# mLSTM layer: one merged query-key map instead of two, and gate products in four 32-column groups

## The reference, cut to what matters

```python
def mlstm_branch(u, conv_w, conv_b, w_q, w_k, w_v, w_gates, b_gates, mh_norm_w, skip_w):
    c = jax.nn.silu(centred_depthwise_conv(u, conv_w, conv_b))
    q = headwise(c, w_q)
    k = headwise(c, w_k)
    v = headwise(u, w_v)
    qkv = jnp.concatenate([q, k, v], axis=-1)
    gates = jnp.einsum('bsc,ncg->nbsg', qkv, w_gates) + b_gates      # 2 directions x 8 gates
    ...
    s = jnp.einsum('bhtd,bhsd->bhts', qj, kj) * jnp.exp(log_D - m_t[..., None])
    ...
    out = h * mh_norm_w + skip_w * c
```

## Time and profile before

| | |
|---|---|
| time, median of 3 runs | 1830.76 us (1828.91 to 1831.51) |
| the profiled execution | 1830.13 us, of it 1828.3 us span |
| TensorE (PE) busy | 1692.8 us, 93% of the span |
| VectorE (DVE) busy | 1047.2 us, 57% |
| ScalarE (ACT), GpSimd (POOL) busy | 585.4 us, 575.0 us |
| mean granted TensorE clock | 0.974 of full |

### The profile page before, as it was taken

The page is one execution under the profiler, slowest core; times in us unless marked ns, Lnnn a source line. Parts: engine busy times, 40 slices in busy tenths (PEclk is TensorE's granted clock), DMA queues, the critical chain, the costliest instruction groups (busy, mean ns, idle before and its releaser), DMA issues.

```text
span 1828.3 us, 20608 instructions
## 1 busy us (share of the span) xinstructions
PE 1692.8 (93%) x8180; PEld 1339.7 (73%) x8180; DVE 1047.2 (57%) x1503; ACT 585.4 (32%) x926; POOL 575.0 (31%) x244
## 2 busy tenths in 40 slices
PE   5899998979988889999999999998899999999996
PEld 4678646557767767778788887886678788887885
DVE  6991224475896467762655555447864555556444
ACT  4212333344311344443322222224343322222223
POOL 2344301125432200003344443443301444444443
PEclk9999999999988999999999999999899999999998
DMA  6222201104221100001223222222201222232231
GB/s 228 72 92 92 81 1 35 35 23 179 81 75 52 47 13 1 1 1 69 81 92 104 93 96 88 93 95 90 82 1 35 81 100 97 92 104 92 81 103 47
DMA packets 37567, 133.75 MB, mean 73 GB/s; under 512 B 4560, under 2 KB 4960, under 8 KB 36960
## 3 DMA queue, kind: packets, MB, share of 16 engines
q1 hardware_dynamic: 34992, 123.22, 19.3%
q10 hardware_dynamic: 2480, 9.22, 1.4%
HBM read 130.33 MB, written 2.10 MB: 72 GB/s over the span
## 4 chain that ended last, share of the span: by engine, by line
PE 78%; DVE 15%; ACT 3%; issue 2%; POOL 1%; ACTq 0%; DMA 0%; DVEq 0%; POOLq 0%
PE ps L1313 15%; PE ps L1315 15%; PE ps L1314 15%; PE ps L1572 5%; PE ps L1612 4%; PE ps L1614 4%; PE ps L1613 4%; PE ps L1540 3%; PE ps L1555 3%; PE ps L1340 2%; DVE sb_arena L776 2%; DVE sb_arena L796 1%; DVE sb_arena L1004 1%; PE ps L1544 1%; PE ps L1414 1%
## 5 line engine op out<-in xcount | busy, mean ns | idle before, releaser
L323 POOL TENSOR_TENSOR sb_w_lo<-sb_raw,sb_w_hi 128x1024 fp32r<-128x1024 f32 x227 | 556.8, 2453 | 1215.8 <-ACT sb_w_hi L357 1215.8
L1313 PE MATMUL ps<-sb_x_hi,sb_w_hi 128*128 128x512 f32 x1464 | 583.9, 399 | 63.4 <-DVE sb_arena L983 17.2
L1314 PE MATMUL ps<-sb_x_lo,sb_w_hi 128*128 128x512 f32 x1464 | 576.3, 394 | 0.0
L1315 PE MATMUL ps<-sb_x_hi,sb_w_lo 128*128 128x512 f32 x1464 | 576.0, 393 | 0.0
L357 ACT CAST sb_w_hi<-sb_raw 128x1024 fp32r<-128x1024 f32 x227 | 238.7, 1052 | 724.1 <-PE ps L1315 540.7
L1313 PEld LDWEIGHTS ps<-sb_x_hi,sb_w_hi 128*128 128x128 f32 x1464 | 278.9, 190 | 136.8 <-issue 20.5
L1315 PEld LDWEIGHTS ps<-sb_x_hi,sb_w_lo 128*128 128x128 f32 x1464 | 278.9, 191 | 59.6
L1314 PEld LDWEIGHTS ps<-sb_x_lo,sb_w_hi 128*128 128x128 f32 x1464 | 279.3, 191 | 57.9 <-issue 1.5
L1200 DVE TENSOR_TENSOR sb_x_lo<-sb_arena,sb_x_hi 128x512 fp32r<-128x512 f32 x44 | 97.6, 2229 | 117.3 <-ACT sb_x_hi L633 117.3
L1612 PE MATMUL ps<-sb_x_hi,sb_w_hi 128*128 128x512 f32 x352 | 139.1, 395 | 8.7 <-DVE sb_x_lo L1200 8.7
L1613 PE MATMUL ps<-sb_x_lo,sb_w_hi 128*128 128x512 f32 x352 | 138.7, 394 | 0.0
(11 more groups left out here) (234 smaller groups left out, 1608.3 us busy)
## 6 DMA issues: line engine op xcount, KB each, us to landing
sb_raw<-in_w SPq DMA_DIRECT2D x227, 512.0 KB, 3.2
sb_resid<-in_x SPq DMA_DIRECT2D x8, 256.0 KB, 6.0
sb_arena<-in_cmp_w1k ACTq DMA_DIRECT2D x1, 2048.0 KB, 9.5
sb_arena<-in_cmp_w1v ACTq DMA_DIRECT2D x1, 2048.0 KB, 15.3
out<-sb_resid SPq DMA_DIRECT2D x8, 256.0 KB, 2.1
sb_arena<-in_pool_w ACTq DMA_DIRECT2D x1, 1024.0 KB, 5.2
sb_arena<-in_invc ACTq DMA_DIRECT2D x1, 1024.0 KB, 7.2
sb_arena<-in_wg ACTq DMA_DIRECT2D x1, 768.0 KB, 8.4
```

The lines of the kernel that those rows point to most:

```text
L323: nc.gpsimd.tensor_tensor(WL[:, w % SPL], raw[:, w % RAW], WH[:, w % SPL].bitcast(F32), ALU.subtract).then_inc(tile_split, 1)
L1313: mm(out, WH[:, s, k], XH[:, k], start=(k == 0), stop=False)
L1314: mm(out, WH[:, s, k], XL[:, k], start=False, stop=False)
L1315: ins = mm(out, WL[:, s, k], XH[:, k], start=False, stop=(k == KT - 1))
```

## The change

Since the scores are products of k = Wk c and q = Wq c, they are (Wq Wk^T c) . c: the change forms the product of the two maps once on the chip and applies it to `c` for the stationary side; the moving side is `c` itself.

- VectorE, `set_up(4)`: two more instructions, which transpose `BD[0]` and `BD[1]` in blocks of 32 x 32 (both are block-diagonal, so this is the whole transpose). `set_up(5)`: one more memset, of the gate weights `wgm`, whose entries are now 32 wide and half zero.
- TensorE, behind tiles 12 and 14 of "in": `merge_maps`, four matmuls of 128 columns each, into bank 7. ScalarE copies each result over `BD[0]` (`QK`), behind its `high(15)` and `high(17)`.
- K/V stage: one product per tile in place of two, with banks 2 and 3 in turn, and its copy on ScalarE. The gate products come behind every second tile, four together: each has 32 stationary columns and writes its own 32 partitions of bank 7 (32q to 32q + 31). The placing matmul then sums the four groups: its matrix `place_w` holds `place` four times, which takes four DMAs where there was one, and zeros between, which takes a memset on GpSimd.
- Head scores: `C` is the moving side in place of `Q1`, so the multiplications by the skip weight must follow the scores. `times_skip(h)` handles tiles 2h and 2h + 1, two per head, and the last two come behind head 3's exponentials, ahead of the root.

```diff
-                                  (place_w[0:16], "place")):
+                                  *[(place_w[32 * q:32 * q + 16], "place") for q in range(4)]):
                     act.dma_start(dst, a[name]).then_inc(consts_in, 16)
...
             for j in range(1, 32):
                 high(j + 2)
+                if j in (13, 15):
+                    n = (j - 13) // 2
+                    act.wait_ge(qk_mm, n + 1)
+                    nc.scalar.copy(QK[:, 4 * n:4 * n + 4].rearrange("p k a b -> p (k a b)"), psum(7)).then_inc(qk_out, 1)
...
+            def times_skip(h):
+
+                act.wait_ge(s_mm1, NT * (h + 1))
+                for j in range(2 * h, 2 * h + 2):
+                    nc.scalar.mul(C[:, j], C[:, j], col("skip", j)).then_inc(skip_ready, 1)
...
-                    for j in range(3 * h, min(3 * h + 3, KT)):
-                        nc.scalar.mul(C[:, j], C[:, j], col("skip", j)).then_inc(skip_ready, 1)
-
+                    times_skip(h)
+
+            times_skip(HEADS - 1)
             act.wait_ge(var_ready, 1)
...
+                if j == 4:
+                    dve.wait_ge(bd_ready, 2)
+                    for n in range(2):
+                        nc.vector.transpose(BDT[n].rearrange("p k c -> p (k c)"), BD[n].rearrange("p k a b -> p (k a b)")
+                                            ).then_inc(bdt_ready, 1)
...
+                    step.mark(nc.vector.memset(wgm, 0.0))
...
+            def merge_maps(n):
+
+                pe.wait_ge(bdt_ready, 2)
+                if n == 1:
+                    pe.wait_ge(qk_out, 1)
+                for j in range(4 * n, 4 * n + 4):
+                    ins = mm(PS[:, 7, P * (j % 4):P * (j % 4) + P], BDT[1][:, j], BDT[0][:, j], start=True, stop=True)
+                ins.then_inc(qk_mm, 1)
...
             for j in range(KT):
                 pe.wait_ge(c_ready, j + 1)
-                for n in range(2):
-                    if j >= 1:
-                        pe.wait_ge(q_out, 2 * (j - 1) + n + 1)
-                    mm(psum(2 + n), BD[n][:, j].rearrange("p a b -> p (a b)"), C[:, j], start=True, stop=True).then_inc(q_mm, 1)
+                if j >= 2:
+                    pe.wait_ge(k_out, j - 1)
+                mm(psum(2 + j % 2), QK[:, j].rearrange("p a b -> p (a b)"), C[:, j], start=True, stop=True).then_inc(k_mm, 1)
...
-                mm(PS[0:16, 7, :], wgm[:, j], C[:, j], start=(j == 0), stop=False)
-                ins = mm(PS[0:16, 7, :], wgm[:, 16 + j], U[:, j, UPAD:UPAD + S], start=False, stop=(j == KT - 1))
+                if j % 2 == 1:
+                    for q in range(4):
+                        n = j - 1 + q // 2
+                        ins = mm(PS[32 * q:32 * q + 32, 7, :], wgm[:, 16 * (q % 2) + n], U[:, n, UPAD:UPAD + S] if q % 2 else C[:, n],
+                                 start=(j == 1), stop=(j == KT - 1))
```

More of the change, by code:

```diff
@@ L168, in build @@
         C = carve(o_c, KT, S)
-        Q1, K1 = carve(o_q, KT, S), carve(o_k, KT, S)
-        pooled, SZ = Q1, K1
+        K1 = carve(o_k, KT, S)
+        pooled, SZ = carve(o_q, KT, S), K1
         V1 = carve(o_v, NT, HEADS, 257)
@@ L174, in build @@
         BD = [carve(o_b + 1024 * i, KT, 32, 4) for i in range(3)]
-        wgm = carve(o_b + 3072, 24, 16)
+        QK = BD[0]
+        BDT = [carve(o_k + KT * P * n, KT, P) for n in range(2)]
+        wgm = carve(o_b + 3072, 24, 32)
         PW = [carve(o_b, 1280), carve(o_b + 1280, 1280)]
@@ L266, in build @@
         pooled_ready, sz_ready, pool_mm, yp_ready = sem("pooled_ready"), sem("sz_ready"), sem("pool_mm"), sem("yp_ready")
-        q_mm, q_out, vt_mm, vt_out, gate_mm, g16 = (sem(x) for x in ("q_mm", "q_out", "vt_mm", "vt_out", "gate_mm", "g16"))
+        k_mm, k_out, vt_mm, vt_out, gate_mm, g16 = (sem(x) for x in ("k_mm", "k_out", "vt_mm", "vt_out", "gate_mm", "g16"))
+        qk_mm, qk_out, bdt_ready = sem("qk_mm"), sem("qk_out"), sem("bdt_ready")
         g_placed, f_rest, nm_ready, fm_ready, emt_ready, cols_mm, acol_ready = (
@@ L319, in _ @@
             nc.gpsimd.memset(eps, EPS).then_inc(zero_set, 1)
+            nc.gpsimd.memset(place_w, 0.0).then_inc(zero_set, 1)
             for w in range(NW):
@@ L388, in _ @@
                 square(0, k)
-            act.wait_ge(zero_set, 2)
+            act.wait_ge(zero_set, 3)
             constants()
@@ L413, in _ @@
             for j in range(KT):
-                act.wait_ge(q_mm, 2 * j + 1)
-                nc.scalar.copy(Q1[:, j], psum(2)).then_inc(q_out, 1)
-                act.wait_ge(q_mm, 2 * j + 2)
-                nc.scalar.copy(K1[:, j], psum(3)).then_inc(q_out, 1)
+                act.wait_ge(k_mm, j + 1)
+                nc.scalar.copy(K1[:, j], psum(2 + j % 2)).then_inc(k_out, 1)
             act.wait_ge(gate_mm, 1)
-            nc.scalar.activation(G16[0:16], PS[0:16, 7, :], ACT.Identity, bias=cols[0:16, COLS["b_gates"]:COLS["b_gates"] + 1]
-                                 ).then_inc(g16, 1)
+            nc.scalar.activation(G16, psum(7), ACT.Identity, bias=col("b_gates")).then_inc(g16, 1)
             act.wait_ge(g_placed, 1)
@@ L754, in set_up @@
                 if j == 1:
-                    dve.wait_ge(consts_in, 16 * 10)
+                    dve.wait_ge(consts_in, 16 * 13)
                 if 1 <= j <= 3:
@@ L803, in _ @@
                 b = product("in", 16 + j)
+                if j == 0:
+                    dve.wait_ge(qk_mm, 2)
                 nc.vector.tensor_tensor(SZ[:, j], psum(b), rstd[:], ALU.mult).then_inc(freed, 1)
@@ L809, in _ @@
                     step.wait()
-                    step.mark(nc.vector.tensor_reduce(wgm, wg.rearrange("p (x o) g -> p x g o", o=4), AX.X, ALU.add))
+                    step.mark(nc.vector.tensor_reduce(wgm[:, :, 0:16], wg.rearrange("p (x o) g -> p x g o", o=4), AX.X, ALU.add))
                     step.wait()
-                    nc.vector.tensor_tensor(wgm[:, 0:8], wgm[:, 0:8], wgm[:, 8:16], ALU.add).then_inc(bd_ready, 1)
+                    nc.vector.tensor_tensor(wgm[:, 0:8, 0:16], wgm[:, 0:8, 0:16], wgm[:, 8:16, 0:16], ALU.add).then_inc(bd_ready, 1)
             dve.wait_ge(bd_ready, 4)
@@ L1012, in _ @@
                 nc.vector.tensor_tensor(VC[:, j], psum(product("nsa", j)), rstd[:], ALU.mult).then_inc(freed, 1)
-            dve.wait_ge(consts_in, 16 * 15)
+            dve.wait_ge(consts_in, 16 * 18)
             rotary_tables = [(csr, cs), (snr, sn)]
@@ L1251, in _ @@
             step.mark(nc.vector.memset(VS[:, :, :, DH:DH + 1], 1.0))
-            dve.wait_ge(consts_in, 16 * 17)
+            dve.wait_ge(consts_in, 16 * 20)
             t0 = T0["swa"]
@@ L1323, in linear @@
                         two_norms() if q == 2 else norm(q)
+                    if stage == "in" and j in (12, 14):
+                        merge_maps(j // 14)
             def turn_values(n, src, ready, value, bank_free):
@@ L1339, in head_scores @@
                     for e in range(2):
-                        ins = mm(psum(2 + j), K1[:, 2 * h + e, P * j:P * (j + 1)], Q1[:, 2 * h + e], start=(e == 0), stop=(e == 1))
+                        ins = mm(psum(2 + j), K1[:, 2 * h + e, P * j:P * (j + 1)], C[:, 2 * h + e], start=(e == 0), stop=(e == 1))
                     ins.then_inc(s_mm1, 1)
+            def merge_maps(n):
[5 more added lines that the diff above has]
+                ins.then_inc(qk_mm, 1)
             linear("in", 32, 0)
@@ L1368, in _ @@
                 ins.then_inc(vt_mm, 1)
-                mm(PS[0:16, 7, :], wgm[:, j], C[:, j], start=(j == 0), stop=False)
-                ins = mm(PS[0:16, 7, :], wgm[:, 16 + j], U[:, j, UPAD:UPAD + S], start=False, stop=(j == KT - 1))
+                if j % 2 == 1:
[3 more added lines that the diff above has]
+                                 start=(j == 1), stop=(j == KT - 1))
             ins.then_inc(gate_mm, 1)
             pe.wait_ge(g16, 1)
-            mm(psum(6), place_w[0:16], G16[0:16], start=True, stop=True).then_inc(g_placed, 1)
-            pe.wait_ge(q_out, 2 * KT)
+            mm(psum(6), place_w, G16, start=True, stop=True).then_inc(g_placed, 1)
+            pe.wait_ge(k_out, KT)
             pe.wait_ge(vt_out, KT)
@@ L1443, in _ @@
             pe.wait_ge(xb_ready, 32)
-            pe.wait_ge(consts_in, 16 * 15)
+            pe.wait_ge(consts_in, 16 * 18)
             for kv in range(2):
```

1 line of the change is left out of this document (added).

## The result

| | before | after |
|---|---|---|
| time, median (range) | 1830.2 us (1828.6 to 1831.5, 6 runs) | 1817.8 us (1815.8 to 1818.6, 6 runs) |
| ratio | | 0.9932, 95% interval 0.9919 to 0.9945 |
| span of the profiled execution | 1828.3 us | 1815.1 us |
| TensorE busy | 1692.8 us | 1679.6 us |

The change makes the kernel 12.4 us faster. I had forecast 8.5 us (1822.3), with a range that ended at 1818.0, 0.2 us above what came: the direction is right, the gain is a third larger than the sum gave.

The account below looks back on a forecast made before the run. Bounds: VectorE in "in", TensorE in the K/V stage, a ScalarE-VectorE-ScalarE chain behind head 3's exponentials. Terms 1.6 + 3.3 - 15.3 + 1.3 + 0.9 = -8.2 us gave a forecast of 1822.3 us, range 1818.0 to 1832.0.

Parts of the forecast that it names:

- DMAs on ScalarE: Start of "in": three more issues of 0.53 us delay the reciprocal, +1.6 us on the path (ends 1.4 and 1.7).
- VectorE's set-up, meetings at zero: In "in": two transposes and a memset, +3.3 us on the path; meetings with GpSimd taken as zero, ends -1 and +2.
- merges on TensorE: Behind tiles 12 and 14 of "in": 2.0 us of matmuls, costed at nothing, covered by TensorE's lead over VectorE.
- K/V stage with its share of clock: K/V stage: bias starts at 248.7 against 264.0, -15.3 us; half a slow stretch behind the new 3 us wait, +0.9.
- skip multiplications: Behind head 3's exponentials: two of 0.66 us each ahead of the root VectorE waits for, +1.3 us on the chain.
- Y: K/V stage: time of four gate products on separate column groups, taken as 1.1 us, with 0.9 to 1.5 as ends.
- the pair on different row halves: Two f32 64x512 matmuls took 1.06 us against 1.82 serially; taken to show independent array parts work at once.
- B: Rival, K/V gates: half-way overlap, four products take five records, Y = 2.15, +4.2 us, 1826.5 us; chance 0.11.
- C: Rival, K/V gates: no overlap of column groups, 3.6 us a set, +10.0 us, 1832.3 us; chance 0.21.
- A: The forecast itself, 1822.3 us, column groups running side by side; own range 1818.5 to 1825.5 us; chance 0.60.
- The clock: K/V stage's start: TensorE's new 3 us wait gets half a slow stretch at 1.2 GHz, +0.9 us.
- D: Rival: clock falls in the K/V stage and stays at 1.2 GHz, +16.2 us, 1838.5 us; chance 0.04.

Follow-up runs that it names:

- e2: Kernel before plus only the gate products in four 32-column groups (wider zeroed weights, three more DMAs), queries and keys still by two products: 1823.3 us, ratio 0.9954.
- f2: Changed kernel with ScalarE's thirteen DMAs issued behind the root of the first norm instead of ahead of it: 1812.9 us.
- f3: Changed kernel with ScalarE's last two skip multiplications behind the root of the variances instead of ahead of it: 1815.4 us.
- e4: Changed kernel with all sixteen gate products, as wide as before, adding up on one group, partitions 0 to 31: 1828.6 us.
- g3: Changed kernel without the K/V start wait, DMAs and last skip multiplications behind their roots, two block-diagonal map products ahead of the reciprocal: 1808.7 us.
- e3: Changed kernel with the gate products put back to two of 16 columns per tile and one DMA of the placing matrix: 1823.8 us, ratio 0.9962.

## Why the prediction was right in direction and short by 4 us

| step | forecast | measured | by |
|---|---|---|---|
| DMAs on ScalarE | +1.6 | +1.4 | reciprocal, three profiles each; e2; f2 |
| VectorE's set-up, meetings at zero | +3.3 | +1.0 | tile 16 less reciprocal, three profiles each; busy time |
| merges on TensorE | 0 | 0 | no wait for them |
| K/V stage with its share of clock | -14.4 | -14.2 | 37.98 to 23.78 |
| skip multiplications | +1.3 | +0.5 to +0.8 | head 3 in three profiles each; f3 |
| clock behind it | 0 | about -1 by the medians | what is left of -12.4 |

**The K/V stage** came as reckoned, by its parts too: Y = 1.00 where I took 1.1, the values of tile 1 a fixed step behind VectorE's first copy (0.73 us, the 0.67 of the copy in it), the bias 16.9 us behind them in f2 and f3 and 18.4 with the stretch of half clock (17.2 forecast, and 0.9 for the clock). The argument from the pair on different row halves carried over to column groups. With it fall B (2.15 a set) and C (3.6). e4 shows C's price, 3.55, for products on one group. The Trainium skill, TensorE: Matmul & The Clock Gate, on packing small matmuls, gives 2.38 times for three groups; the runs show 3.55 us against 1.00 for four in f32, 3.55 times. B took the same section's strict order of starts and ends to mean that each product's second record must start ahead of the next product's first. The trace doesn't contradict the order, but it does contradict that premise: the eight records of a set start one behind the other, first four 7 ns apart (241.780 to 241.800 us), then the other four (242.233 to 242.253), which I take for the first and then the second records of four products. The pair of the earlier trace rows, which I had held against the rule, starts in the same way (756.781 and .787, then 757.314 and .321). So the order of starts does not imply B's time; the ends of matmuls are modelled in these traces and decide nothing.

**The step that failed** is the term of the set-up: "I take zero and keep both ends". The instructions were priced rightly (2.37 and 0.70 us), but the meetings of VectorE and GpSimd took 2.1 us back, twice what my end allowed (-1). The rows already held the size: the operation of the earlier trace rows took 2.61 us where the same one takes 0.55 unmet, and it ended just behind the subtraction (62.97 and 62.69 us). One meeting missed or added is worth up to 2 us, not 1, every other one changes its price with the alignment, and some 15 stand ahead of tile 16. The sign could not be had from the profile of before. What I could have had is the width: -2 to +2, which would have put the low end at 1817.

Two other things belong to the miss. The measured steps alone, -11.2 us from the median of six runs of before, give 1819.0 us, inside the range; it took the last row of the table as well, which no run assigns to a cause, to bring 1817.8. And the range of A doesn't follow from its terms: the ends written for Y, the meetings and the clock add up to -2.7 and +4.5 us, 1819.6 to 1826.8, and not to 1818.5 and 1825.5. That the whole range missed by only 0.2 us is luck of that sum.

**The skip multiplications** had the right wait (3.20 us; 3.3 forecast), and a second effect that I didn't look for: L936 no longer met a subtraction, which gave 0.46 us back. It is the same kind of meeting as in "in".

**The clock**: 0.9 for the new wait was fair (1.5 us in four of seven). What was missing is that the whole tail varies by some 3 us between executions of one program. Of the 13.2 us by which the two first spans differ, 1.7 is such chance and can't be credited to the change.

The measured steps ahead of the last row sum to -11.2 us; the medians differ by 12.4. The 1.2 between is within the interval of the ratio (2.4 us each way).

**D and the slower side** did not come: half clock lasted one stretch of 3.4 us and not the stage, in each profile that had it.

## What to carry to other kernels

Small f32 products with at most 32 stationary columns are worth putting on four column groups even at the price of zeroed weights and extra copies of a table: here 2.55 us per four. Where VectorE is the bound and GpSimd works beside it, don't sum prices of VectorE's instructions to better than the price of one meeting (up to 2.2 us here); look at time to the next fixed point, and at VectorE's busy time up to it, in several profiles instead. Where a short VectorE operation takes several times its usual time, look first at what GpSimd does just then. And before crediting a saving, compare the part of the program that didn't change: here it varied by more than most single edits were worth.

## What the runs showed of the hardware that I had not expected

- Four f32 products of 512 columns on four groups take 1.00 us, on one group 3.55: their first records start 7 ns apart (241.780, .787, .793 and .800 us). One alone took 0.91.
- An operation of VectorE on SBUF alone that starts under a GpSimd subtraction is held until the subtraction ends, however short it is (a cast of 0.22 us took 1.90, a tap of 0.55 took 2.61, L936's 0.17 became 0.64). The other way round, a subtraction that starts under such an operation takes longer (2.35 to 3.35 us in g3). The reciprocal of `rstd` kept its 3.35 us beside two subtractions. VectorE's operations that read PSUM did not: sixteen take 0.63 to 0.69 us in "in", four of them (44.4, 99.2, 122.1, 128.6 us) beside a running GpSimd subtraction.
- The same 3.1 us of VectorE work cost 3.3 us alone, with the reciprocal at 29.3 to 29.9, and 1.0 in the whole change, with it at 30.7 to 31.0, each three times out of three. The start alone doesn't decide: in e3 the 2.4 us of transposes, with the reciprocal at 29.4 and without the memset, cost 1.0 as well.
- Two kernels that differ by nothing behind 138 us had tails that differ by 4 us in two profiles of three. For most of it the places of the stretches of half clock account; what sets these is left open.
